# A two-layer token pool and a 31-tap convolution computed in another way: group weights before the window, and four shifted copies per product

## The reference, cut to what matters

```python
def conformer_conv(h, w_pw1, b_pw1, w_dw, b_dw, ln_g, ln_b, w_pw2, b_pw2):
    a, gate = jnp.split(h @ w_pw1 + b_pw1, 2, axis=-1)
    u = a * jax.nn.sigmoid(gate)
    u = lax.conv_general_dilated(u, w_dw[:, None, :], ..., padding=((CONV_WIDTH - 1, 0),),
                                 feature_group_count=D_MODEL) + b_dw
    u = jax.nn.silu(layer_norm(u, ln_g, ln_b))
    return u @ w_pw2 + b_pw2

def multiscale_pool(h, w_group, scale):
    for gi, w in enumerate(POOL_WINDOWS):
        xg = hg[:, :, gi, :]
        cs = jnp.cumsum(xg, axis=1)
        cs_shift = jnp.pad(cs, ((0, 0), (w, 0), (0, 0)))[:, :L]
        outs.append((cs - cs_shift) / count - xg)
    mixed = jnp.einsum("blgc,gcd->blgd", pooled, w_group)
    return mixed.reshape(B, L, D_MODEL) * scale

hn = rms_norm(h, mix_norm_g[0]); h = h + conformer_conv(hn, ...)
hn = rms_norm(h, ffn_norm_g[0]); h = h + swiglu(hn, ...)
hn = rms_norm(h, mix_norm_g[1]); h = h + multiscale_pool(hn, ...)
hn = rms_norm(h, ffn_norm_g[1]); h = h + moe_swiglu(hn, ...)      # 8 experts, top 2
```

## Time and profile before

| | us |
|---|---|
| median of three runs (2128.88 to 2129.3) | 2129.07 |
| the profiled execution | 2130.01 |
| its span, first to last instruction | 2128.2 |
| PE busy in the span | 2047.7 (96%) |
| DVE busy | 1533.0 (72%) |
| ACT busy | 1207.0 (57%) |

### The profile page before, as it was taken

One profiled execution on the slowest core, in us unless ns is written; L12 is line 12 of the kernel. 1 busy time (PEld: TensorE's weight loads), 2 busy tenths in 40 slices (PEclk: granted clock), 3 DMA queues, 4 the chain that ended last, 5 costly groups with the idle time before them and its releaser, 6 DMA issues.

```text
span 2128.2 us, 31732 instructions
## 1 busy us (share of the span) xinstructions
PE 2047.7 (96%) x12232; PEld 1801.2 (85%) x12232; DVE 1533.0 (72%) x1729; ACT 1207.0 (57%) x1357; POOL 52.6 (2%) x94
## 2 busy tenths in 40 slices
PE   7989999799999999999999999999999989999997
PEld 6979999687888888888878888889978869989997
DVE  5976562789898898888889898896576157626653
ACT  6554442467777676776777777675354246515442
POOL 2000000000000000000000000001000100020000
PEclk8999999799999999999999999999999989999999
DMA  4214444099898998989989898994432324444551
GB/s 190 80 71 168 179 178 159 29 348 362 326 354 337 345 370 314 366 337 344 346 338 366 326 354 337 347 368 150 179 139 93 128 77 159 159 159 170 187 179 60
DMA packets 70102, 504.19 MB, mean 237 GB/s; under 512 B 7680, under 2 KB 8704, under 8 KB 8832
## 3 DMA queue, kind: packets, MB, share of 16 engines
q1 hardware_dynamic: 70016, 502.95, 63.0%
HBM read 501.87 MB, written 1.05 MB: 236 GB/s over the span
## 4 chain that ended last, share of the span: by engine, by line
PE 86%; DVE 7%; ACT 4%; issue 2%; DMA 1%; POOL 0%; DVEq 0%; ACTq 0%; POOLq 0%; SPq 0%
PE ps L541 8%; PE ps L544 8%; PE ps L545 8%; PE ps L748 8%; PE ps L752 8%; PE ps L751 8%; PE ps L773 5%; PE ps L777 4%; PE ps L776 4%; PE ps L518 3%; PE ps L1033 2%; PE ps L602 2%; PE ps L1036 2%; PE ps L1035 2%; DVE ring_r L1693 2%
## 5 line engine op out<-in xcount | busy, mean ns | idle before, releaser
L1693 DVE TENSOR_TENSOR ring_r<-ring,high 128x2048 fp32r<-128x2048 f32 x227 | 517.6, 2288 | 98.2 <-ACT high L1351 92.3
L1351 ACT ACTIVATE high<-ring 128x2048 fp32r<-128x2048 f32 x224 | 428.5, 1913 | 16.5 <-DMA ring<-w_stream 16.4
L1559 DVE TENSOR_TENSOR ring_r<-ring,high 128x2048 fp32r<-128x2048 f32 x120 | 274.2, 2287 | 128.5 <-ACT high L1213 128.1
L751 PE MATMUL ps<-ring_r,big_r 128*128 128x512 f32 x896 | 349.0, 389 | 0.0
L544 PE MATMUL ps<-scr_r,high 128*128 128x256 f32 (+1 forms) x1200 | 344.2, 287 | 0.0
L1213 ACT ACTIVATE high<-ring 128x2048 fp32r<-128x2048 f32 x120 | 228.5, 1908 | 158.6 <-PE ps L541 87.9
L748 PE MATMUL ps<-high,big_r 128*128 128x512 f32 x704 | 288.1, 409 | 0.0
L752 PE MATMUL ps<-high,big_r 128*128 128x512 f32 x704 | 275.5, 391 | 0.0
L1693 DVE TENSOR_TENSOR ring_r<-ring,scr_r 128x2048 fp32r<-128x2048 f32 x112 | 254.8, 2287 | 5.6 <-ACT scr_r L1351 1.0
L541 PE MATMUL ps<-sq_r,high 128*128 128x272 f32 (+1 forms) x832 | 239.8, 288 | 7.6 <-DVE scr_r L1566 7.6
L545 PE MATMUL ps<-sq_r,ring_r 128*128 128x272 f32 (+1 forms) x832 | 238.7, 287 | 0.0
(11 more groups left out here) (405 smaller groups left out, 3793.7 us busy)
## 6 DMA issues: line engine op xcount, KB each, us to landing
ring<-w_stream SPq DMA_DIRECT2D x477, 1024.0 KB, 4.8
h<-h_in SPq DMA_DIRECT2D x1, 1088.0 KB, 5.1
out<-hn SPq DMA_DIRECT2D x1, 1024.0 KB, 4.7
vec<-vec_in SPq DMA_DIRECT2D x1, 576.0 KB, 8.0
```

The costliest lines, as they stand in the source:

```text
L751: pe.matmul(o, x_item_high[:, k, :], w_low[:, cols], start=False, stop=False)
L1351: act.activation(w_high, w, ACT.Copy).then_inc(S["moe_high"], 1)
L1559: dve.tensor_tensor(w_low, blocks_at(c, 0, CH), w_high.bitcast(F32), ALU.subtract).then_inc(S["weights_low"], 1)
L1693: dve.tensor_tensor(w_low, w, w_high.bitcast(F32), ALU.subtract).then_inc(S["moe_low"], 1)
```

## The change

The convolution leaves DVE. For each tile SP copies the gate product into `shifted`: for each group of 32 channels, four copies one token apart lie on the four quarters of the partitions (16 DMAs of 32 rows a tile). A product over 128 partitions then covers four taps of 32 channels, and eight steps cover 32 taps (the 32nd is zero); the stationary matrix is 128x32 and holds four diagonals. The four groups write the four quarters of the same PSUM bank. DVE forms all 32 small matrices of a tile in one instruction, from `w_dw` laid out anew on the host. PE does the convolution of tile j - 2 behind pair j.

The pooling is reordered: since group weights, window and the norm's per-token root commute, PE first multiplies the residual `h` of each group by the group weights (scaled with the norm's gain on ACT), with tokens as rows, between and behind the output pairs of the feed-forward layer. The window is then a banded 128x128 matrix over tokens, one for each width, formed on POOL; the root of each token scales its rows. Three overlapping ranges of tokens (128, 128 and 46) cover the 272. The pool weights move ahead of `ffn0_out` in the stream. The first three expert chunks are split beside the last output pair, the sums of squares are added on DVE before one-column products, and some steps of the expert choice change places: the table is made later and with two instructions instead of nine, and the second item copy moves from DVE to ACT.

```diff
-PE_TAPS = [13] * 6 + [15, 16]
+TURNS = 4
+GROUPS = P // 32
+TAP_STEPS = -(-CONVW // TURNS)
+CONV_PAD = TURNS * TAP_STEPS - CONVW
+CONV_LEN = CONVW - 1 + T0 + CONV_PAD
+SHIFT_LEN = T0 + TURNS * (TAP_STEPS - 1)
...
-    ("pw1", 8 * KD), ("pw2", 4 * KD), ("ffn0_in", KF * KD), ("ffn0_out", 4 * KF), ("pool", 8),
+    ("pw1", 8 * KD), ("pw2", 4 * KD), ("ffn0_in", KF * KD), ("pool", 8), ("ffn0_out", 4 * KF),
...
+        shifted = big[:, 7680:7680 + 3 * GROUPS * SHIFT_LEN].rearrange("p (b g t) -> p b g t", b=3, g=GROUPS)
...
+        rows_of = ((0, P, META, P - 16), (P - 15, P, P, P - 15), (2 * P - 30, 46, 2 * P - 15, 31))
+        pool_w = hn[:, :, :].rearrange("p k t -> p (k t)")[:, 0:KD * WIDE].rearrange("p (k d) -> p k d", k=KD)
+        pool_rows = scr[:, 0:3 * D].rearrange("p (n d) -> p n d", n=3)
+        band = scr[:, 4352:4352 + 4 * P].rearrange("p (g t) -> p g t", g=4)
+        bands = sq[:, :, :].rearrange("p k t -> p (k t)")[:, 0:12 * P].rearrange("p (n g t) -> p n g t", n=3, g=4)
...
+            def shift(j):
+                sp.wait_ge(S["glu_done"], j + 1)
+                if j >= 3:
+                    sp.wait_ge(S["conv_done"], j - 2)
+                if j:
+                    sp.wait_ge(S["shift_landed"], 16 * GROUPS * TURNS * j)
+                for g in range(GROUPS):
+                    for s in range(TURNS):
+                        sp.dma_start(shifted[32 * s:32 * s + 32, j % 3, g, :],
+                                     conv_u[32 * g:32 * g + 32, j, s:s + SHIFT_LEN]).then_inc(S["shift_landed"], 16)
             turns_pre = C_MOE // RING
-            with sp.Fori(1, turns_pre) as r:
+            for c in range(RING, 3 * RING):
...
+                sp.wait_ge(pre_begun, c - RING + 2)
+                sp.dma_start(slot(c), w_stream[c]).then_inc(dense_landed[c % RING], 16)
+                if c - RING < KD - 1:
+                    shift(c - RING)
+                if c - RING == KD - 2:
+                    shift(KD - 1)
...
             def conv_tile(j):
-                pe.wait_ge(S["glu_done"], j + 1)
+                pe.wait_ge(S["shift_landed"], 16 * GROUPS * TURNS * (j + 1))
                 pe.wait_ge(S["diag_ready"], j + 1)
                 claim(6)
-                for tap in range(PE_TAPS[j]):
-                    mm = pe.matmul(ps[:, 6, 0:T0], diag[:, j % 2, tap, :], conv_u[:, j, tap:tap + T0],
-                                   start=(tap == 0), stop=(tap == PE_TAPS[j] - 1))
+                for n in range(TAP_STEPS):
+                    for g in range(GROUPS):
+                        mm = pe.matmul(ps[32 * g:32 * g + 32, 6, 0:T0], diag[:, j % 3, g * TAP_STEPS + n, :],
+                                       shifted[:, j % 3, g, TURNS * n:TURNS * n + T0],
+                                       start=(n == 0), stop=(n == TAP_STEPS - 1))
                 mm.then_inc(S["conv_done"], 1)
...
-                if j >= 1:
-                    conv_tile(j - 1)
                 if j >= 2:
-                    add_to_mean(j - 2)
+                    conv_tile(j - 2)
+                if j >= 3:
+                    add_to_mean(j - 3)
+            conv_tile(6)
+            add_to_mean(5)
             conv_tile(7)
...
+                if n == 0:
+                    pe.wait_ge(S["normed"], normed_at(3, KD - 1))
...
-                    if j == 2:
-                        sum_tiles(3 if n == 0 else 10, t, range(4))
-                sum_tiles(3 if n == 0 else 10, t, range(4, KD))
-            ffn(0, 2, 2, T0, in_low_ffn0, hid_high0, hid_low0, BOFF["ffn0_in"], BOFF["ffn0_out"])
+                    behind(j)
...
+            def pool_products(g):
+                pe.wait_ge(S["ffn_out"], 2 * g + 2)
+                if g:
+                    pe.wait_ge(S["pooled"], 2 * g)
+                for n, (t0, rows, _, _) in enumerate(rows_of):
+                    o = ps[0:rows, 6 + n // 2, (n % 2) * WIDE:(n % 2 + 1) * WIDE]
+                    if g == 3 and n == 2:
+                        token_sums(3, 0, rows_of)
+                    for k in range(2):
+                        mm = pe.matmul(o, h[:, 2 * g + k, t0:t0 + rows], pool_w[:, 2 * g + k, :],
+                                       start=(k == 0), stop=(k == 1))
+                mm.then_inc(S["pool_done"], 1)
+            def token_sums(i, bank, tiles):
+                claim(bank)
+                pe.wait_ge(S["sq_summed"], SUMMED.index(i) + 1)
+                for n, (t0, rows, *_) in enumerate(tiles):
+                    mm = pe.matmul(ps[0:rows, bank, n:n + 1], squares_of(i)[:, 0, t0:t0 + rows], ones[:, 0:1],
+                                   start=True, stop=True)
+                mm.then_inc(S["sum_done"], 1)
+            def pool_inside(j, k):
+                if j == 3 and k == 6:
+                    pool_products(2)
+            def pool_behind(j):
+                if j in (1, 2):
+                    pool_products(j - 1)
+            ffn(0, 2, 2, T0, in_low_ffn0, hid_high0, hid_low0, BOFF["ffn0_in"], BOFF["ffn0_out"],
+                pool_inside, pool_behind)
+            pool_products(3)
+            bank_owner.clear()
...
+            pe.wait_ge(S["bands_ready"], 2)
+            for m in range(KD):
+                g, cols = m // 2, slice(m * P, (m + 1) * P)
+                if m >= 4:
+                    pe.wait_ge(S["x_ready"], KD + m - 3)
+                if m == 6:
+                    pe.wait_ge(S["pooled"], 8)
+                for n, (t0, rows, o0, outs) in enumerate(rows_of):
+                    mm = pe.matmul(ps[:, m % 4, o0 - META:o0 - META + outs], pool_rows[0:rows, n, cols],
+                                   bands[0:rows, n, g, o0 - t0:o0 - t0 + outs], start=True, stop=True)
+                mm.then_inc(S["pool_done"], 1)
+                if m >= 2:
+                    route(m - 2)
+            for m in (6, 7):
+                route(m)
+            token_sums(4, 5, ((0, P), (P, P)))
...
-                for tap in range(PE_TAPS[j]):
-                    ins = act.activation(diag[:, j % 2, tap, :], ident[:, :], ACT.Copy,
-                                         scale=vcol("w_dw", j * CONVW + tap))
-                ins.then_inc(S["diag_ready"], 1)
...
+            def scale_pool(k):
+                if k == 0:
+                    wait_landed(act, C_POOL, None)
+                act.activation(pool_w[:, k, :], blocks_at(C_POOL, k, k + 1), ACT.Copy, scale=vcol("mix_g1", k))\
+                   .then_inc(S["normed"], 1)
...
+                        if n == 0 and p >= KF - 4:
+                            scale_pool(2 * (p - KF + 4))
+                            scale_pool(2 * (p - KF + 4) + 1)
...
+            for k in range(4):
+                squares3(k)
+            take_last(0)
+            squares3(4)
+            squares3(5)
+            split_first(0)
+            take_last(1)
+            split_first(1)
+            take_last(2)
+            split_first(2)
+            act.activation(warm, eps_col, ACT.Sqrt)
+            squares3(6)
+            squares3(7)
+            act.wait_ge(S["sum_done"], 4)
+            act.activation(root3[:, 0:2], ps[:, 0, 0:2], ACT.Sqrt, bias=eps_col, scale=1.0 / D)
+            act.activation(root3[0:46, 2:3], ps[0:46, 0, 2:3], ACT.Sqrt, bias=eps_col[0:46, :], scale=1.0 / D)\
+               .then_inc(S["std_ready"], 1)
+            act.wait_ge(S["consts_ready"], 3)
+            act.wait_ge(S["root_col_ready"], 1)
+            act.activation(bands[:, 1], band, ACT.Copy, scale=root3[:, 1:2]).then_inc(S["bands_ready"], 1)
+            take_last(3)
...
+            act.wait_ge(S["pick_done"], 2)
+            act.activation(x_item_low.rearrange("p (b k) c -> p b (k c)", b=2), ps[:, 0:2, :], ACT.Copy)\
+               .then_inc(S["pick_low"], 1)
...
+            step(dve.tensor_reduce(diagonal, ident[:, :].rearrange("p (b c) -> p c b", c=32), AX.X, ALU.add))
+            def make_diag(j):
+                if j >= 3:
+                    dve.wait_ge(S["conv_done"], j - 2)
+                n = GROUPS * TAP_STEPS
+                dve.tensor_tensor(diag[:, j % 3, :, :], diagonal.unsqueeze(1).broadcast_to([P, n, 32]),
+                                  vcol("w_dw", j * n, n).unsqueeze(2).broadcast_to([P, n, 32]), ALU.mult)\
+                   .then_inc(S["diag_ready"], 1)
...
+                dve.tensor_scalar(conv_y[:, j, :], ps[:, 6, 0:T0], vcol("b_dw", j), None, ALU.add)\
+                   .then_inc(S["conv_ready"], 1)
...
+                if j >= 3:
+                    take_conv(j - 3)
+                make_diag(j)
...
+            def take_rows(g):
+                dve.wait_ge(S["pool_done"], g + 1)
+                dve.tensor_copy(pool_rows[:, 0:2, g * WIDE:(g + 1) * WIDE],
+                                ps[:, 6, :].rearrange("p (t d) -> p t d", t=2)).then_inc(S["pooled"], 1)
...
+            def pool_beside(m):
+                if m == 3:
+                    take_rows(0)
+                if m == 5:
+                    add_squares(3, (1, 2, 3))
+                    split_low(0, 1)
```

(48 more changed lines are left out.)

210 lines of the change are left out of this document (103 added, 107 removed).

## The result

The changed kernel takes 2142.07 us, the median of its five executions, and the kernel before, timed beside it, takes 2129.3 us. One of the five took 3384.62 us at a granted clock of 0.554 and is left out of what follows. The other four took 2141.71 to 2143.03, which is 1.0058 times as long as before, 95% interval 1.0045 to 1.0072. The forecast was 2094 us, in a range of 2085 to 2121: wrong in sign, and by 48 us.

A forecast was written before the change was run, and what follows sets the result against it. It took PE to bound the convolution, weight products and expert loop, and a serial chain at low clock the pooling. 2130.0 - (17.9 + 17.2 = 35.1) = 2094.9 profiled, 0.9 less for the median: 2094.0 us, range 2085 to 2121.

The forecast's parts named there:

- The products: Convolution on PE: the 32-column matmuls of four column groups overlap fully, 4.0 us a tile, ends 3.5 and 14.6.
- only neighbours overlap: Rival in the convolution: passes start strictly in program order, 7.3 us a tile, 2119 us in all; chance 0.14.
- The copies: Convolution stage: SP's 16 DMAs a tile take 8.6 us with the weight chunk, hidden behind PE's 10.5 except at both ends.
- d: Time from start to start of SP's copy issues in the convolution stage, taken as 0.42 us.
- The rival: SP becomes the convolution's bound: 2109 us at 0.56 us between issues; chance 0.12 below 0.73, 0.04 beyond.
- the pool gain: Pooling and routing stage: 25.3 us gained behind the output half, less 8.1 lost in it, 17.2 us.
- The period of 10.5: Convolution stage: PE sets the pace of a tile, 6.0 + 4.0 + 0.46 = 10.5 us.
- The group weights: Feed-forward layer: PE waits 2.1 us for scaled pool weights, three product groups add 7.8; output half ends 8.1 us later.
- The tail: Pooling and routing behind the output half: 27.0 us where it took 52.3, ends 24 and 34.
- a rival with 0.08: The clock falls in the eight tiles of the pool stage: 2101 us in all; chance 0.08.
- The expert loop finds five chunks in the ring as before and moves forward whole: Expert loop: it starts earlier with nothing giving the gain back there, so no loss was counted.
- The sum: Whole kernel: gains of 17.9 us in the convolution and 17.2 in the pooling, 35.1 together.

## Why the prediction was wrong, point by point

- **The products**: right. 3.87 us for 64 passes (4.0 forecast, 3.5 and 14.6 the ends), a quarter of the 14.6 that they would take one after the other; "only neighbours overlap" (0.14), with 7.3, fell. The 4.6 us that came from the Trainium skill, page TensorE: Matmul & The Clock Gate, Part 3, is too much here, and by the strict order of that page a second pass would hold back the next group, which isn't seen.
- **The copies, the step that failed**: "I take d = 0.42, nearer the quiet row since each moves 38 KB and not 1 MB". The size of a DMA was taken as what counts, and the copies over 128 partitions show that it isn't. Of the two rows, the one of issues in a row (0.56 apart) was the like one, for the copies come in rows of 16; the quiet 0.333 belongs to issues that come alone. The rival had the formula: 36.9 + 8 x (15d + 2.25) + 5.3 gives 136.3 with the 0.634 of the first tile and 139.4 with the mean of 0.66; measured 138.3. It had 0.16 in all, with its turning point at d = 0.73 on the ground that all else stood. But the 10 us behind 425, 9.3 in the tail and 3 in the output half make 5.1 us more than the 17.2 of the pool gain. The change is then faster only if the stage ends by 130.7 - 5.1 = 125.6, which the same formula has at about d = 0.55. The period of 10.5, the start and the end of the stage were right, as 111.3 for 112.8 shows where the issues are out of the way (weight chunks there at 69.28, 79.73 and 90.19, so 10.45 a tile).
- **The group weights**: the wait was 2.13 (2.1 forecast), a group of products 2.72 (2.6). Missing was the clock of 0.50 behind the wait, about 2 us; "The waits of these groups I put at nothing" held but for some 0.3 us ahead of each of the three.
- **The tail**: 27.0 forecast, 36.3 measured from 388.5 to the loop at 424.83. Two terms were too small. The larger is the clock: 0.50 from about 397 to 414, a rival with 0.08 whose argument, "PE idles 1.4 us ahead of them and no longer 5", looked at waits, while the clock falls with the waits filled too. The other is the six band passes of a tile: 0.93 us at full clock (0.43 forecast from the columns alone), with four of the router 0.36 (0.44). An estimate from these rows: eight tiles take 8 x (0.93 + 0.36) = 10.3 us at full clock where 8.7 was forecast, so 1.6 of the 9.3 are the passes and most of the rest is the clock. And 21.8 for the end of the filler matmuls is 0.8 more than its own terms, 16.4 and 4.56, add up to; the small products between them, which it doesn't name, take 0.6 here (414.56 to 415.15).
- **"The expert loop finds five chunks in the ring as before and moves forward whole"**: wrong, by 10 us. A loss here was put at nothing because nothing new is waited for; the place of `big` slows an iteration from 127.56 to 129.12 us. The new length of the taps stands in the first lines of the diff.
- **The sum**: 25.5 + 3 + 9.3 + 10 = 48. The rivals were priced one at a time, each as if the rest of the sum stood, and 2121 was the end for one of them; two came true together and a loss came on top that no rival had.

## What to carry over

Price small DMAs by their issue on the queue that issues them, per DMA and from rows in which as many come in a row, and count the issues as work of that engine: what is queued behind them waits. Look at what a change does to the addresses of tiles it never names: eight columns in a table cost about 9 us here in a loop that starts almost 300 us after the convolution, and an unused tile gave them back. A stretch of narrow products can run at half the clock with no gap in it; here a wide product that nobody reads was cheaper than none, by 3.7 us.

## What the runs showed of the hardware that was not expected

- With the tile that holds the loop's 128x128 stationary operands at 32 or 64 bytes past a multiple of 128, counted from the first tile, an iteration of matmuls of 512 columns took 1.2 and 1.0% longer (129.1 and 128.87 us for 127.56), at 395 and 394 ns for 389 in the mean of one.
- An issue of a copy within memory costs its engine 0.59 to 0.60 us in the middle, whether of 32 rows or of 128, and the weight chunk right behind such copies 0.58 for 0.33. Two engines' queues issue side by side: eight copies in 4.97 us on one and eight in 5.29 on the other at the same time, where sixteen on one took 10.0 to 11.1.
- The granted clock fell from 1.00 to 0.50 within a stretch in which PE's rows show no gap at all (busy 4.00 of 4 us), and stayed at 1.00 in the same tiles with one product of 256 columns added to each.
